# Small table operands in PSUM, phase angles ahead of GpSimd's tables, and the direct term first in block 0 of a state-space front

## The reference, cut to what matters

```python
hn = rmsnorm(h, norm_mix[0])                      # u = hn
dt = exp(log_dt);  mag = exp(lam_re * dt)
a_r, a_i = mag * cos(lam_im * dt), mag * sin(lam_im * dt)
coef = ((a_r - 1) + 1j * a_i) / (lam_re + 1j * lam_im)
bb = coef * (b_re + 1j * b_im)                    # input matrix
x[t] = a * x[t - 1] + bb @ u[t]                   # per group
y[t] = Re(c @ x[t]) + d * u[t]
a, b = split(gelu(y) @ w_glu);  h = h + a * sigmoid(b)
```

## Time and profile before

| | |
|---|---|
| median of 3 runs | 2080.7 us |
| lowest and highest | 2079.78 and 2086.28 us |
| the profiled execution | 2082.57 us, its span 2080.8 us |
| granted PE clock, mean | 0.975 |
| PE busy | 1947.3 us (94%), 9494 instructions |
| DVE busy | 1268.3 us (61%) |
| ACT busy | 900.5 us (43%) |
| POOL busy | 430.1 us (21%) |
| chain that ended last | PE 76%, DVE 9%, ACT 5%, POOL 3% |

### The profile page before, as it was taken

How to read it: one execution, slowest core, us unless ns; L and a number is a source line. 1 busy time by engine, 2 the same in 40 slices (tenths; PEclk the granted TensorE clock), 3 DMA queues, 4 the chain that set the end, 5 groups by cost and what they waited for, 6 DMA issues and landing times.

```text
span 2080.8 us, 27316 instructions
## 1 busy us (share of the span) xinstructions
PE 1947.3 (94%) x9494; PEld 1565.4 (75%) x9494; DVE 1268.3 (61%) x1783; ACT 900.5 (43%) x1507; POOL 430.1 (21%) x295
## 2 busy tenths in 40 slices
PE   3889999999999967999999999999999998999996
PEld 1668788888887745788888887878878886777774
DVE  7873443343469587543343468987667765777764
ACT  3674432232334255432332333445445552366661
POOL 5672200000043010300000043342212224000003
PEclk8899999999999979999999999999999999999998
DMA  4113332333332200333333332222222222212221
GB/s 178 44 34 111 91 101 91 101 92 100 95 98 90 83 1 11 92 101 93 98 97 95 101 91 81 82 61 67 66 81 64 69 72 62 90 61 63 69 72 61
DMA packets 54522, 166.98 MB, mean 80 GB/s; under 512 B 13216, under 2 KB 13344, under 8 KB 53920
## 3 DMA queue, kind: packets, MB, share of 16 engines
q1 hardware_dynamic: 54432, 165.78, 26.6%
HBM read 161.30 MB, written 2.10 MB: 79 GB/s over the span
## 4 chain that ended last, share of the span: by engine, by line
PE 76%; DVE 9%; ACT 5%; POOL 3%; issue 2%; DMA 2%; DVEq 0%; POOLq 0%; SPq 0%; PEldq 0%; ACTq 0%
PE bank L183 15%; PE bank L184 15%; PE bank L185 15%; PE bank L1501 4%; PE bank L1502 4%; PE bank L1503 4%; PE bank L2107 2%; DMA raw<-in_w_dram 2%; PE bank L2109 2%; PE bank L2108 2%; PE bank L1516 1%; POOL acc L234 1%; PE bank L1517 1%; PE bank L1518 1%; ACT w_hi L195 1%
## 5 line engine op out<-in xcount | busy, mean ns | idle before, releaser
L203 DVE TENSOR_TENSOR w_lo<-raw,w_hi 128x1024 fp32r<-128x1024 f32 x286 | 366.8, 1282 | 466.2 <-ACT w_hi L195 465.0
L195 ACT ACTIVATE w_hi<-raw 128x1024 fp32r<-128x1024 f32 x289 | 305.8, 1058 | 627.3 <-DMA raw<-in_w_dram 627.2
L183 PE MATMUL bank<-x1h,w_hi 128*128 128x512 f32 x744 | 291.6, 392 | 6.5 <-DVE x1l L218 6.5
L185 PE MATMUL bank<-x1h,w_lo 128*128 128x512 f32 x744 | 289.8, 389 | 0.0
L184 PE MATMUL bank<-x1l,w_hi 128*128 128x512 f32 x744 | 289.7, 389 | 0.0
L183 PE MATMUL bank<-x0h,w_hi 128*128 128x512 f32 x704 | 277.9, 395 | 0.0
L185 PE MATMUL bank<-x0h,w_lo 128*128 128x512 f32 x704 | 274.1, 389 | 0.0
L184 PE MATMUL bank<-x0l,w_hi 128*128 128x512 f32 x704 | 274.0, 389 | 0.0
L232 POOL TENSOR_TENSOR sq<-h 128x512 f32 (+1 forms) x64 | 79.0, 1234 | 783.2 <-DVEq L940 659.7
L183 PEld LDWEIGHTS bank<-x1h,w_hi 128*128 128x128 f32 x744 | 139.7, 188 | 38.0 <-DVE x1l L218 7.8
L184 PEld LDWEIGHTS bank<-x1l,w_hi 128*128 128x128 f32 x744 | 139.8, 188 | 29.3 <-issue 0.7
(11 more groups left out here) (382 smaller groups left out, 3457.3 us busy)
## 6 DMA issues: line engine op xcount, KB each, us to landing
raw<-in_w_dram SPq DMA_DIRECT2D x289, 512.0 KB, 3.6
h<-in_xT_dram SPq DMA_DIRECT2D x1, 2048.0 KB, 13.0
Ur<-in_xu_dram SPq DMA_DIRECT2D x8, 256.0 KB, 2.7
out_dram<-h SPq DMA_DIRECT2D x8, 256.0 KB, 2.2
const<-in_const_dram SPq DMA_DIRECT2D x1, 1028.0 KB, 13.9
B_st<-in_B_dram SPq DMA_DIRECT2D x1, 1024.0 KB, 7.7
C_st<-in_C_dram SPq DMA_DIRECT2D x1, 1024.0 KB, 15.1
p_in<-in_pT_dram SPq DMA_DIRECT2D x1, 1024.0 KB, 4.8
```

What stands on the lines that cost most here:

```text
L183: e.matmul(b, w_hi[:, w, k], xh[:, k], start=(k == 0), stop=False)
L185: last = e.matmul(b, w_lo[:, w, k], xh[:, k], start=False, stop=(k == KT - 1))
L195: e.activation(w_hi[:, z], raw[:, z], ACT.Copy).then_inc(hi_split, 1)
L203: e.tensor_tensor(w_lo[:, z], raw[:, z], w_hi[:, z].bitcast(F32), ALU.subtract).then_inc(w_split, 1)
```

## The change

**Bank 3 as a store for small operands.** `w`, `ci` and `ru` get columns in it (`w_col`, `ci_col`, `ru_col`), as do the product `d_gain` and the powers of block 0 (`first_powers`). So the instructions that read them beside an SBUF tile have one operand in SBUF and one in PSUM. ACT writes the powers of block 0 in a new copy, for which `psi_ready` is now counted up twice: after `PB` is complete, which releases ACT, and after `psi`, which releases POOL. `ru_col` is a new copy on DVE. The norm's square root is written in place in its PSUM bank, and the product with `sel` goes to SBUF (`sq`).

**Copies and small products moved.** `mag8` goes from behind `c_powers` to right behind `psi`. The product for `DI` goes ahead of `PB`, and `DI` itself ahead of the norm's product.

**POOL** forms the angles of block 1 ahead of the tables of block 1. **PE** computes the direct term of block 0 ahead of `step_sums`, and ACT keeps it ahead of `Sx`.

```diff
 # GpSimd
-            e.wait_ge(psi_ready, 1)
+            e.wait_ge(psi_ready, 2)
...
             for T in range(NBLK + 2):
+                if T == 0:
+                    angles(T + 1)
                 if 0 <= T + 1 < NBLK:
                     tables(T + 1)
...
-                if 0 <= T + 1 < NBLK:
+                if 0 < T and T + 1 < NBLK:
                     angles(T + 1)
 # ScalarE
             e.wait_ge(psi_ready, 1)
+            e.activation(first_powers, PB[:, :, 0:GB, 0:STEP], ACT.Copy).then_inc(powers_kept, 1)
             keep_powers(e, 1)
...
-            act_norm(e, 0, eps6)
+            e.wait_ge(norm_mm, 1)
+            e.activation(bk[4], bk[4], ACT.Sqrt, bias=eps6[:, :], scale=1.0 / DM).then_inc(sd_ready, 1)
...
                     turned(T)
+                    k_kept(T)
                     s_kept(T)
-                    k_kept(T)
...
+        w_col, ci_col, ru_col = (bank[3][:, 64 * i:64 * i + 64] for i in range(3))
+        d_gain = bank[3][0:SH, 192:256]
+        first_powers = bank[3][:, 256:384].rearrange("p (r g s) -> p r g s", r=2, g=GB)
 # VectorE
             link(e, e.reciprocal(v("den"), v("den")))
+            link(e, tt(d_gain, V("d_h", rows=SH), V("gain_u", rows=SH), ALU.mult))
...
             link(e, tt(PB[:, 0], mag, power["cos"][:, :, :], ALU.mult))
+            e.sem_inc(psi_ready, 1)
             link(e, ts(psi[:, :], power["turns"][:, :, STEP], 1.0, None, ALU.mult))
             e.sem_inc(psi_ready, 1)
+            link(e, ts(mag8[:, :], mag[:, :, STEP], 1.0, None, ALU.mult))
...
-                if q:
-                    e.wait_ge(powers_kept, 1 if q <= 4 else 2)
-                kept = [powers(r, (q - 1) % 4) if q else cut(PB[:, r], q)[:, :, 0:STEP] for r in range(2)]
+                e.wait_ge(powers_kept, (q + 3) // 4 + 1)
+                kept = [powers(r, (q - 1) % 4) if q else first_powers[:, r] for r in range(2)]
...
-                wr, ci = over(v("w")[:, lo:hi]), over(v("ci")[:, lo:hi])
+                wr, ci = over(w_col[:, lo:hi]), over(ci_col[:, lo:hi])
...
-            link(e, ts(v("w"), v("c1"), V("nsgn"), None, ALU.mult))
+            link(e, ts(w_col, v("c1"), V("nsgn"), None, ALU.mult))
...
-            link(e, tt(v("ci"), v("c3"), v("c2"), ALU.subtract))
+            link(e, tt(ci_col, v("c3"), v("c2"), ALU.subtract))
             c_powers(0, GB)
             c_powers(GB, SG)
-            link(e, ts(mag8[:, :], mag[:, :, STEP], 1.0, None, ALU.mult))
...
             fractions(0)
+            dfull = [SH, SG, SH]
+            link(e, tt(DI[:, :, :], d_gain.unsqueeze(2).to_broadcast(dfull), C("id16", rows=SH).unsqueeze(1).to_broadcast(dfull), ALU.mult))
             e.wait_ge(sd_ready, 1)
...
-            ru3 = bk[7].rearrange("p (c s) -> p c s", s=STEP)
-            link(e, tt(ru3, sd[:, :].rearrange("p (c s) -> p c s", s=STEP), C("sel").unsqueeze(1).to_broadcast(rf), ALU.mult))
+            ru3 = sq[:, :].rearrange("p (c s) -> p c s", s=STEP)
+            link(e, tt(ru3, bk[4].rearrange("p (c s) -> p c s", s=STEP), C("sel").unsqueeze(1).to_broadcast(rf), ALU.mult))
...
+            link(e, ts(ru_col, ru[:, :], 1.0, None, ALU.mult))
             e.wait_ge(u_loaded, 16)
-            s5_inputs.took("U", tt(Ub[:, 0], Ur[:, :, :], ru[:, :].unsqueeze(1).to_broadcast(full), ALU.mult))
-            dg = bank[7][0:SH, 0:SG]
-            link(e, tt(dg, V("d_h", rows=SH), V("gain_u", rows=SH), ALU.mult))
...
+            s5_inputs.took("U", tt(Ub[:, 0], Ur[:, :, :], ru_col.unsqueeze(1).to_broadcast(full), ALU.mult))
 # TensorE
                 if T == 0:
                     transposed(T)
+                    direct(T)
                     step_sums(T)
                     rotated(T)
-                    direct(T)
```

More of the change, by code:

```diff
@@ L697, in s5_vector @@
             e.sem_inc(ru_ready, 1)
+            link(e, ts(ru_col, ru[:, :], 1.0, None, ALU.mult))
             e.wait_ge(u_loaded, 16)
-            s5_inputs.took("U", tt(Ub[:, 0], Ur[:, :, :], ru[:, :].unsqueeze(1).to_broadcast(full), ALU.mult))
-            dg = bank[7][0:SH, 0:SG]
-            link(e, tt(dg, V("d_h", rows=SH), V("gain_u", rows=SH), ALU.mult))
-            dfull = [SH, SG, SH]
-            link(e, tt(DI[:, :, :], dg.unsqueeze(2).to_broadcast(dfull), C("id16", rows=SH).unsqueeze(1).to_broadcast(dfull), ALU.mult))
+            s5_inputs.took("U", tt(Ub[:, 0], Ur[:, :, :], ru_col.unsqueeze(1).to_broadcast(full), ALU.mult))
             e.wait_ge(b_gained, 2)
```

## The result

The changed kernel takes 2063.27 us, the median of 5 executions (2060.53 to 2064.81); the kernel before, beside it, 2080.7 (5 executions, 2077.93 to 2086.28). The profiled execution of after has a span of 2061.5 us. One execution of a later run, e9, took 6450 us, for a reason that nothing here shows, and is left out of its median.

The account below looks back on a forecast made before the run. It took PE to bound most of the kernel, with DVE's waits on PE and POOL delaying the state-space layer's front. The scan's copy 17.1 us earlier, less 0.5 for a new lock, gave 16.6: 2064 from the median 2080.7, range 2058 to 2071.

Follow-up runs that it names:

- e9: e4 plus a wait: POOL's second table product of a block is held until DVE's rotation two blocks earlier is done; 2067.93 us, ratio 0.9934.
- e8: e7 plus the hold of e9, with POOL's order at block 1 set to tables, angles, inputs; 2061.67 us, ratio 0.9914.
- f2: e8 measured once more, unchanged; 2064.65 us, ratio 0.9922.
- e4: The changed kernel with POOL's order undone (tables of block 1, inputs, then angles of block 1); 2070.12 us, ratio 0.9937.
- e7: e5 with the gain on block 0's part of the input matrix (line 681) put ahead of psi on DVE; 2060.51 us, ratio 0.9903.
- e5: The changed kernel with the copy mag8 made by ACT, ahead of the sines, instead of by DVE; 2068.03 us, ratio 0.9926.
- e3: The changed kernel with the columns w and ci put back from the PSUM bank to SBUF; 2072.19 us, ratio 0.9946.
- e1: The kernel before with only block 0's direct term moved ahead of the step sums on PE and kept ahead of Sx on ACT; 2077.46 us, ratio 0.9973.

## What to carry to other kernels

Where VectorE and GpSimd both work, look for an instruction of VectorE whose time is bimodal (0.69 and 1.8 to 3.0 here): put its small operand into a PSUM bank, or start it while GpSimd idles. In a loop that repeats, read who is first at each such meeting and by how much, and look at it again in all blocks behind an edit to the order. If the margin is tenths of a microsecond, a semaphore that holds GpSimd back for the length of one instruction secures it in the trace (0.70 in every block of e8, e9 and f2); that it also lowers the median is not shown here. Before a median is explained, compare the kernels at a mark inside the trace, and before a trace is explained, see where its execution stands among the others: e4's was the slowest of six.

## What the hardware showed that wasn't expected

- The lock goes both ways, and small instructions take part: two instructions of 64 columns from SBUF to SBUF took 1.10 (line 633, after) and 1.17 (line 687, e7) behind POOL, where such a one took 0.21 unhindered (line 687, e5); POOL's products of 1152 columns took 2.57 (line 428, after) and 2.65 (line 427, e3) for 2.14 where DVE had been first.
- A lost meeting can recur and need not. In e4 DVE's rotation waited in blocks 0 to 5 (1.69 to 2.68 us), in e1, e5 and e7 in block 0 alone (1.96, 2.33 and 1.56; 0.89 in block 1 of e7), and in before in block 3 alone (2.17), where DVE was first again one block later by 0.02 (113.75 against 113.77).
- Two executions of the kernel before dropped TensorE's clock to half at the same instruction (85.48 and 85.38), but got it back after different times, at 96.0 and 89.0: the steps were 15.8 and 13.8 us.
